# Two-block transformer-like kernel on one core: output projection and second up chunk of the second block by seven half-size products, with an up chunk's weight sums placed between the projection's additions

## The reference, cut to what matters

```python
def _layer(x, positions, g_mix, w_in, b_forget, w_branch, w_out, g_mlp, w_up, w_down):
    h = _rmsnorm(x, g_mix)
    proj = h @ w_in
    ...
    gates = jax.nn.sigmoid(gl.reshape(b, s, N_BRANCH, D_MODEL))
    y = (gates[:, :, 0, :] * (br_a @ w_branch[0])
         + gates[:, :, 1, :] * (br_b @ w_branch[1])
         + gates[:, :, 2, :] * (br_c @ w_branch[2]))
    x = x + y @ w_out                                  # 1024 x 1024: the output projection

    h2 = _rmsnorm(x, g_mlp)
    x = x + jnp.square(jax.nn.relu(h2 @ w_up)) @ w_down   # 1024 x 4096 and 4096 x 1024
    return x
```

## Time and profile before

| | us |
|---|---|
| median of 3 runs | 1498.56 (1496.29 to 1503.31) |
| the profiled execution | 1495.67, of which its span is 1493.9 |
| PE busy in the span | 1431.2 (96%) |
| DVE, ACT, POOL busy | 823.0, 328.2, 279.7 |
| mean granted TensorE clock | 0.985 of full speed |
| layer 1's branches, output projection and first two up chunks | 723.57 to 822.02 |
| the same of layer 2 | 1214.31 to 1312.77 |

### The profile page before, as it was taken

The page is one execution under the profiler, slowest core; times in us unless marked ns, Lnnn a source line. Parts: engine busy times, 40 slices in busy tenths (PEclk is TensorE's granted clock), DMA queues, the critical chain, the costliest instruction groups (busy, mean ns, idle before and its releaser), DMA issues.

```text
span 1493.9 us, 31093 instructions
## 1 busy us (share of the span) xinstructions
PE 1431.2 (96%) x13529; PEld 1279.6 (86%) x13529; DVE 823.0 (55%) x1495; ACT 328.2 (22%) x685; POOL 279.7 (19%) x144
## 2 busy tenths in 40 slices
PE   5999999989989899999999999999999999999997
PEld 2777877878778799998888999999999888899986
DVE  2345355566562666767335674544776733566553
ACT  1104023434433310143200120002014430012100
POOL 3502210000000077634000000005764400000000
PEclk8899999999989999999999999999999999999999
DMA  9533012001111464333344444446443334444451
GB/s 359 191 113 113 1 32 59 2 18 44 59 60 57 110 215 167 128 124 128 132 138 144 170 170 170 170 128 207 146 168 114 114 129 154 169 165 169 157 180 50
DMA packets 107479, 191.30 MB, mean 128 GB/s; under 512 B 8744, under 2 KB 25856, under 8 KB 107216
## 3 DMA queue, kind: packets, MB, share of 16 engines
q1 hardware_dynamic: 105968, 187.39, 36.4%
q10 hardware_dynamic: 448, 0.66, 0.2%
q0 software_dynamic: 928, 1.26, 0.2%
HBM read 187.32 MB, written 1.05 MB: 126 GB/s over the span
## 4 chain that ended last, share of the span: by engine, by line
PE 90%; DMA 2%; DVE 2%; issue 2%; ACT 1%; DVEq 1%; POOLq 1%; POOL 0%; SPq 0%; ACTq 0%
PE psum L1524 17%; PE psum L1385 15%; PE psum L1360 12%; PE psum L1521 6%; PE psum L1663 5%; PE psum L920 4%; PE psum L1644 4%; PE psum L1381 3%; PE psum L1576 2%; PE psum L993 2%; PE psum L1002 2%; PE psum L1166 2%; PE psum L1226 2%; PE psum L1445 1%; DMA arena<-in_mod_w 1%
## 5 line engine op out<-in xcount | busy, mean ns | idle before, releaser
L2111 ACT ACTIVATE arena<-psum 128x256 f32<-128x256 f32 (+7 forms) x256 | 115.1, 465 | 692.0 <-PE psum L1385 109.1
L1385 PEld LDWEIGHTS psum<-arena 128*128 128x128 f32 x2240 | 254.3, 192 | 10.8 <-issue 8.0
L1385 PE MATMUL psum<-arena 128*128 128x128 f32 x2240 | 261.2, 276 | 2.3 <-DVE arena L2720 1.2
L1524 PEld LDWEIGHTS psum<-arena 128*128 128x128 f32 x2240 | 250.4, 192 | 0.1
L1524 PE MATMUL psum<-arena 128*128 128x128 f32 x2240 | 250.5, 275 | 0.0
L1360 PE MATMUL psum<-arena 128*128 128x256 f32 x896 | 195.6, 379 | 0.0
L1360 PEld LDWEIGHTS psum<-arena 128*128 128x128 f32 x896 | 169.2, 189 | 24.7 <-issue 0.3
L873 POOL TENSOR_TENSOR arena<-arena 128x1024 f32<-128x1024 f32 x12 | 28.5, 2375 | 377.8 <-DMA arena<-in_w_in 360.9
L1521 PE MATMUL psum<-arena 128*128 128x256 f32 x448 | 97.0, 379 | 0.0
L1521 PEld LDWEIGHTS psum<-arena 128*128 128x128 f32 x448 | 84.9, 190 | 11.8
L1663 PE MATMUL psum<-arena 128*128 128x256 f32 x336 | 73.5, 380 | 1.1 <-issue 1.1
(11 more groups left out here) (403 smaller groups left out, 2008.8 us busy)
## 6 DMA issues: line engine op xcount, KB each, us to landing
arena<-in_w_in SPq DMA_DIRECT2D x31, 2048.0 KB, 8.4
arena<-in_w_up SPq DMA_DIRECT2D x16, 2048.0 KB, 8.4
arena<-in_w_down SPq DMA_DIRECT2D x16, 2048.0 KB, 8.0
arena<-in_w_out SPq DMA_DIRECT2D x6, 2048.0 KB, 7.9
arena<-in_w_branch SPq DMA_DIRECT2D x6, 2048.0 KB, 7.9
arena<-in_mod_w SPq DMA_DIRECT2D x5, 2048.0 KB, 13.7
arena<-in_w_in SPq DMA_DIRECT2D x12, 512.0 KB, 4.3
arena<-in_w_in SPq DMA_DIRECT2D x3, 1024.0 KB, 7.0
```

The costliest lines, as they stand in the source:

```text
L1385: mm = pe.matmul(b[:, n * P:(n + 1) * P], left[:, k, n * P:(n + 1) * P], right[:, k, :], start=k == 0, stop=k == half - 1)
L1524: mm = pe.matmul(b[:, n * P:(n + 1) * P], left[:, k, n * P:(n + 1) * P], right[:, k, :], start=first and n == 0 and k == 0, stop=last and ...
L2111: return act.activation(dst, src, ACT.Copy, scale=scale)
```

## The change

Four things change in each of the two layers.
1. The output projection's two chunks go by halves: 2 x 7 products instead of 4 results. Their weight sums are made by POOL, behind the gates' sums (new loop in the GpSimd block), their token sums by DVE behind the last branch addition (into `tok`). PE takes the products in the order 1, 2, 6, 5, 7, 3, 4; `out0_1` waits for `br21`, `out0_2` for `br23`, product 6 for the token sums, products 6, 7 and 3 for the weight sums.
2. ACT copies each half's first product, and DVE combines the seven results into the residual.
3. The second up chunk goes by halves too (`FIRST_SEVEN = 1`), with weight sums on DVE.
4. These weight sums (`weight_sums(0)`) no longer stand behind the token sums of `ht`, but inside the second half's additions: after those for product 7, before those for products 3 and 4.

```diff
@@ constants
-FIRST_SEVEN = 2
+FIRST_SEVEN = 1
+OUT_PRODUCTS = (1, 2, 6, 5, 7, 3, 4)
@@ GpSimd, behind the loop over the gates' chunks
+                    ly.wait_filled(gp, f"o{len(PAIRS) - 1}", l)
+                    for h in range(2):
+                        n = len(FIRST) + N_IN + 3 + h
+                        gp.wait_ge(s_slot[SLOT[n]], l * SLOT_PER_LAYER[SLOT[n]] + landed(n))
...
+                        gp.tensor_tensor(s1, w21, w22, ALU.add)
+                        gp.drain()
+                        gp.tensor_tensor(s2, s1, w11, ALU.subtract)
+                        gp.drain().then_inc(sem("out_weights_summed"), 1)
+                        gp.tensor_tensor(w21, w11, w21, ALU.subtract)
+                        gp.drain().then_inc(sem("out_weights_summed"), 1)
+                        gp.tensor_tensor(s4, w12, s2, ALU.subtract)
+                        gp.drain().then_inc(sem("out_weights_summed"), 1)
@@ TensorE
                 w = use_chunk(pe, n0 + N_IN + 3 + h, l)
-                for n in range(2):
-                    tiles(f"out{2 * h + n}", w, (2 * n * P, (2 * n + 1) * P), src=yy,
-                          ready=(lambda k: ly.wait_emptied(pe, f"br2{k // 2}", l)) if h == 0 and n == 0 else None)
+                for m in OUT_PRODUCTS:
+                    b = take_bank(ly, f"out{h}_{m}", l)
+                    if h == 0 and m < 3:
+                        ly.wait_emptied(pe, f"br2{2 * m - 1}", l)
+                    if m == 6:
+                        pe.wait_ge(sem("out_tokens_summed"), l + 1)
+                    if m in (6, 7, 3):
+                        pe.wait_ge(sem("out_weights_summed"), 3 * (2 * l + h) + (6, 7, 3).index(m) + 1)
+                    product_of_halves(b, w, m, [wsum[:, h, y] for y in range(3)], x=yy, x_sums=tok).then_inc(ly.filled, 1)
@@ ScalarE
-            norm_scalar(act, ly, "ss2", "squares2", l, done, emptied, lambda k: ly.wait_emptied(act, f"out{k // 2}", l))
+            def first_out(h):
+                ly.wait_filled(act, f"out{h}_1", l)
+                if h:
+                    ly.wait_emptied(act, "out0_7", l)
+                emptied(ly, copy(u1, bank(ly, f"out{h}_1", l)[:, 0:T], 0.5))
...
+            norm_scalar(act, ly, "ss2", "squares2", l, done, emptied, residual)
@@ VectorE
-            for n in range(4):
-                ly.wait_filled(dve, f"out{n}", l)
...
-                gained(dve, gains[1], "raw2_ready", (2 * n, 2 * n + 1))
-                if n:
-                    squares_summed(dve, done, fence, "squares2", l, (n - 1,))
-            squares_summed(dve, done, fence, "squares2", l, (3,))
+                    if (b_, n) == (2, 1):
+                        dve.tensor_tensor(tok[:, 0], token_halves(yy)[1], token_halves(yy)[0], ALU.subtract)
+            y11, y12, y21, y22 = token_halves(yy)
+            dve.tensor_tensor(tok[:, 1], y22, tok[:, 0], ALU.subtract)
+            dve.tensor_tensor(tok[:, 2], y22, y12, ALU.subtract)
+            fence()
+            dve.tensor_tensor(tok[:, 3], tok[:, 1], y21, ALU.subtract)
+            done("out_tokens_summed")
...
+            for h in range(2):
...
+                ly.wait_emptied(dve, f"{g}_1", l)
+                emptied_all(half_more(x11, product(g, 2), x11), 1)
+                emptied_all(half_more(v2, product(g, 6), v1), 1)
+                fence()
+                dve.tensor_tensor(x11, x11, v1, ALU.add)
+                p5 = product(g, 5)
+                half_more(v4, p5, v2)
+                half_more(x22, p5, x22)
+                emptied_all(half_more(v3, product(g, 7), v2), 2)
+                fence()
+                dve.tensor_tensor(x12, x12, v4, ALU.add)
+                dve.tensor_tensor(x22, x22, v3, ALU.add)
+                dve.tensor_tensor(x21, x21, v3, ALU.add)
+                fence()
+                if h:
+                    weight_sums(0)
+                    squares_summed(dve, done, fence, "squares2", l, (0, 1))
+                emptied_all(half_more(x12, product(g, 3), x12), 1)
+                fence()
+                gained(dve, gains[1], "raw2_ready", (4 * h, 4 * h + 1))
+                emptied_all(half_more(x21, product(g, 4), x21, -0.5), 1)
+                fence()
+                gained(dve, gains[1], "raw2_ready", (4 * h + 2, 4 * h + 3))
+            squares_summed(dve, done, fence, "squares2", l, (2, 3))
@@ VectorE, behind the normalised tokens
             token_sums(ht, *[tok[:, n] for n in range(4)])
-            weight_sums(0)
```

More of the change, by code:

```diff
@@ L372, in plan_layer @@
             p += [(f"o{i - 1}", "A", 1)]
-    p += [(f"br{b}{n}", "D", 1) for b in range(3) for n in range(4) if b or n] + [(f"out{n}", "D", 1) for n in range(4)]
+    p += [(f"br{b}{n}", "D", 1) for b in range(3) for n in range(4) if b or n]
+    p += [(f"out{h}_{m}", "A" if m == 1 else "D", 1) for h in range(2) for m in OUT_PRODUCTS]
     p += [("ss2", "A", 1), ("up0", "D", 1), ("up1", "D", 1)]
@@ L400 @@
 CHUNK_ENDS = (["qc1", "kf", "vc"] + [f"{x}_4" for x in HEAD_PARTS] + [f"gl{n}_4" for n in range(GATES)]
-              + [f"br{b}3" for b in range(3)] + ["out1", "out3"] + [f"up{2 * n + 1}" if n < FIRST_SEVEN else f"up{n}_4" for n in range(8)]
+              + [f"br{b}3" for b in range(3)] + ["out0_4", "out1_4"] + [f"up{2 * n + 1}" if n < FIRST_SEVEN else f"up{n}_4" for n in range(8)]
               + [None] * 3 + ["dn0_4"] + [None] * 3 + ["dn1_4"])
@@ L1513, in seven @@
                 for m in PRODUCTS:
+                    if i == 0 and m == 1:
+                        pe.wait_ge(sem("h2_ready"), l * KT + half)
                     if m == 6:
+                        if i == 0:
+                            pe.wait_ge(sem("token_sums"), 5 * l + 1)
                         pe.wait_ge(sem("weight_sums"), SEVENS * l + i + 1)
@@ L2899, in layer_vector, with weight_sums @@
             v1, v2, v3, v4 = [two_tiles(v) for v in (u1, u2, u3, u4)]
+            def weight_sums(i):
+                n = len(FIRST) + N_IN + 5 + FIRST_SEVEN + i
+                dve.wait_ge(s_slot[SLOT[n]], l * SLOT_PER_LAYER[SLOT[n]] + landed(n))
+                if SEVENS * l + i >= 2:
+                    dve.wait_ge(sem("sums_read"), SEVENS * l + i - 1)
+                s1, s2, s4 = [wsum[:, i % 2, x] for x in range(3)]
+                w11, w21, w12, w22 = quarters(ring[:, SLOT[n]])
+                dve.tensor_tensor(s1, w21, w22, ALU.add)
+                fence()
+                dve.tensor_tensor(s2, s1, w11, ALU.subtract)
+                dve.tensor_tensor(w21, w11, w21, ALU.subtract)
+                fence()
+                dve.tensor_tensor(s4, w12, s2, ALU.subtract)
+                done("weight_sums")
@@ new lines, in half_more @@
+            def half_more(dst, p, x, sign=0.5):
+                return dve.scalar_tensor_tensor(dst, p, sign, x, ALU.mult, ALU.add)
+            for h in range(2):
+                x11, x12 = [xr[:, 4 * h:4 * h + 2, r] for r in (slice(0, P), slice(P, T))]
+                x21, x22 = [xr[:, 4 * h + 2:4 * h + 4, r] for r in (slice(0, P), slice(P, T))]
+                g = f"out{h}"
+                ly.wait_emptied(dve, f"{g}_1", l)
[16 more added lines that the diff above has]
+                emptied_all(half_more(x12, product(g, 3), x12), 1)
+                fence()
+                gained(dve, gains[1], "raw2_ready", (4 * h, 4 * h + 1))
+                emptied_all(half_more(x21, product(g, 4), x21, -0.5), 1)
+                fence()
+                gained(dve, gains[1], "raw2_ready", (4 * h + 2, 4 * h + 3))
@@ L2976, in hidden_sums @@
                 token_sums(x, hid1[:, q], hid2[:, q], token_halves(x)[1], hid4[:, q])
[L2978 to L2990, removed]
-                dve.tensor_tensor(s4, w12, s2, ALU.subtract)
-                done("weight_sums")
             ly.wait_emptied(dve, "ss2", l)
```

25 lines of the change are left out of this document (11 added, 14 removed).

## The result

| | before | changed |
|---|---|---|
| median | 1497.42 us (1493.24 to 1503.31, 8 runs) | 1508.40 us (1505.56 to 1516.37, 8 runs) |
| ratio | | 1.0071, 95% interval 1.0045 to 1.0098 |
| the profiled execution | 1495.67, span 1493.9, clock 0.985 | 1516.37, span 1514.5, clock 0.979 |

The change makes the kernel slower by 0.7%, 11.0 us.

What follows compares the result with a forecast made beforehand. PE was taken to bound the kernel, busy 1431.2 of 1493.9 us. PE's work -8.1, first wait +6.4, second +6.8, clock +4.5 gave +9.6 on the median 1498.56: 1508.2 us; range 1497 to 1515.5.

Steps and rivals of the forecast that it cites:

- PE's work, -8.1: Output projection and second up chunk by halves: PE saves 4.07 us a layer, 8.1 us in both.
- First wait, 3.2 a layer: Output projection, product 6: PE waits 3.2 us a layer for token sums, as DVE's additions wait out POOL's sums.
- its list of signs: Signs in the new profile: among them, DVE's additions L2914 and L2919 to L2922 last 1 to 2.4 us, not 0.69.
- Second wait, 3.4 a layer: At ss2 (L928), PE waits 3.4 us a layer for DVE's sum of squares; bounds 2.9 to 3.8.
- What costs nothing: POOL's sums for both halves, result banks and everything behind ss2 were to add no wait.
- The cover at product 6 of the second up chunk: Behind ss2, token sums end 8.6 us after it, PE wants them 10.9 us after: 2 us cover.
- The clock, +4.5: Granted clock falls behind the new waits: four occasions of 0 to 3.0 us each, 1.5 counted, +4.5 us.
- The sum: Whole kernel: -8.1 +6.4 +6.8 = +5.1 us, with the clock +9.6, set on median 1498.56: 1508.2 us.
- -0.7 to +5: Rival: POOL's sums miss the token sums, first wait 0.3 instead of 3.2; 1498 to 1503 us; chance 0.12.
- -1.7 without the clock: Rival: the ss2 wait does not come, the first does; -1.7 us, 1497; chance 0.05.
- -7.5: Rival: neither wait comes, gain of the seven products kept; -7.5 us, 1491, faster; chance 0.08.
- both waits with the clock at full speed: Rival: both waits come, the clock stays; +5.1 us, 1503.7; chance 0.22.

Runs made afterwards that it cites:

- the run with the projection alone: Kernel before with only the output projection by halves, POOL's second group of sums behind the token sums: 1491.01 us, ratio 0.9967.
- The runs with one part alone: Kernel before with only the output projection by halves (1491.01 us, 0.9967), or only the second up chunk, weight sums behind the last sum of squares (1495.81 us, 0.9986).
- POOL out of the way: Changed kernel, POOL's second group of sums held until the output projection's token sums are done: 1496.12 us, ratio 0.9996; repeated 1500.04 us, 1.0022.
- The squares in time: Changed kernel with the second up chunk's weight sums moved behind the last sum of squares: 1495.55 us, ratio 0.9997.
- Both together: Changed kernel, POOL's second sums behind the token sums and up chunk's weight sums behind the last sum of squares: 1489.13 us, ratio 0.9942; repeated 1491.42 us, 0.9968.
- the run with the weight sums in their old place: Changed kernel with POOL's second sums held back and the up chunk's weight sums behind the token sums of h2: 1503.95 us, ratio 1.0042.

## Why the prediction was right

1508.2 us was predicted and 1508.4 measured, slower by 0.7%. By its own steps:

- *PE's work, -8.1.* Right in kind, 0.8 too large. The two chunks of the projection cost 25.45 us, not 25.01, so that its share is 2.3 us a layer (38.33 of the 66.06 in the earlier trace rows are the branches' 176 records, by the chain of the run with the projection alone), and the up chunk's 1.35 (188.95 before, 187.60 after, both with all chunks by halves that follow): -7.3 in both layers. The runs with one part alone gave -4.2, with 0.47 us of wait in it, and -2.4: -7.0 without that wait.
- *First wait, 3.2 a layer.* 3.3 and 2.9 measured, for the cause given. Set on the same start of the branches, POOL's last sum ended at 770.9, within the 770.2 to 771.4 worked out, and product 6 started at 773.3, within 772.2 to 773.4. The steps of the prediction lengthen only the first sum behind the last branch addition, its list of signs all three; the second and third took 0.68 and 0.69, so the steps were right and the list was not.
- *Second wait, 3.4 a layer.* 3.50 and 3.56 measured; the four additions are its cause, as the run without them there shows. DVE's order was as worked out: weight sums 801.53 to 806.50, squares done at 811.82, `ss2` at 811.99.
- *What costs nothing.* Held: no wait for banks, for the second half's weight sums, or behind `ss2`. The cover at product 6 of the second up chunk was called 2 us; with the weight sums put there, their 5.1 us overran it by 2.9.
- *The clock, +4.5.* Mis-sized, 6.8 in the profiled layers and 6.6 in the mean over all executions (26.8 less 20.2). It fell on three of four occasions and not on one and a half, at 1.7 or 3.4 us each and not 3.0.
- *The sum.* -7.3 + 6.25 + 7.06 + 6.8 = +12.8 for the profiled layers, which measured +12.7; predicted +9.6. The medians differ by 11.0 in the first comparison and by 16.7 in the second (6 runs of the changed kernel). So the two waits and their causes were foreseen, but that 1508.2 lies so close to 1508.4 is luck. Two terms were off the same way, by 0.8 and 2.3; the base 1498.56, a median of 3 runs, lay 1.1 above the median of 8, which hid as much; and the runs of a median scatter by more.
- *Rivals.* The runs made three of the four come true; both waits with the clock at full speed were seen in none of the changed kernel's two profiles. POOL out of the way gave +5.1 in the layers and no change or +0.2% in the time, against -0.7 to +5. The squares in time gave +1.6 in the layers and no change, against -1.7 without the clock. Both together gave 7.5 and 5.0 us less than the kernel before, against -7.5.

## What to carry to other kernels

When PE's work is cut by half a per cent, the sums that replace it must go where their engine really idles: DVE idled 2.75 us ahead of the reciprocal in the run with the weight sums in their old place, and in the second half it had no idle time between the additions of products 7, 3 and 4. A helper engine that reads SBUF costs nothing only while the other engine's additions of two SBUF operands are not urgent, so order the helper behind the urgent ones rather than start it as early as its data allow. And when you add a wait of PE, allow for the clock behind it: here 13.3 us of waits brought 6.8 us of clock in both profiles of the changed kernel. It is an average and no fixed price, as the last section shows.

## What the hardware showed that I had not expected

- Each fall of the granted clock in the changed part cost 1.7 or 3.4 us, and the same wait of 3.5 us cost the one or the other: held-back POOL lost 3.4 in layer 1 and 1.7 in layer 2 in one execution, and 1.7 and 3.4 in the next. Behind the token sums it fell in layer 1, after waits of 1.21 to 1.36 and 2.09, and not in layer 2, after 1.21 and 1.73 or 1.74, in all four profiles that have these waits. In code that is the same in all kernels, such waits can cost nothing. The wait of 3.48 us before 501.59 of the earlier trace rows, from which the prediction took its 3.0 us, stands in all fourteen profiles: it cost 3.2 to 3.4 us in twelve of them, 1.7 in one and nothing in one, the first with POOL held back.
- Unchanged code makes most of the scatter between executions (1489.6 to 1506.1 for the kernel before). The layer 1 piece measured here began anywhere between 717.66 and 737.22 us, in fourteen profiles and with no order by kernel. One of the places is in the first block. DVE and POOL there, before:

```profile
148.05 0.69 DVE L2449 TENSOR_TENSOR arena<-arena 128x512 f32<-128x512 f32 x1
148.66 0.69 DVE L2451 TENSOR_TENSOR arena<-arena 128x512 f32<-128x512 f32 x1
149.43 2.67 DVE L2453 SCALAR_TENSOR_TENSOR arena<-arena 128x512 f32<-128x512 f32 x1
```

```profile
148.78 2.77 POOL L842 TENSOR_TENSOR arena<-arena 128x1024 f32<-128x1024 f32 x1 [12.28 <-DMA arena<-in_w_in]
```

and after:

```profile
148.12 2.64 DVE L2485 TENSOR_TENSOR arena<-arena 128x512 f32<-128x512 f32 x1
150.68 2.83 DVE L2487 TENSOR_TENSOR arena<-arena 128x512 f32<-128x512 f32 x1
153.60 2.66 DVE L2489 SCALAR_TENSOR_TENSOR arena<-arena 128x512 f32<-128x512 f32 x1
```

```profile
147.60 2.61 POOL L844 TENSOR_TENSOR arena<-arena 128x1024 f32<-128x1024 f32 x1 [11.04 <-DMA arena<-in_w_in]
```

The same three instructions, once one of them slow and once all three. In all fourteen profiles the first slow one is the first that DVE starts after POOL has started its own first sum, even where only 0.01 to 0.04 us lie between the two starts. POOL starts when a transfer of weights has landed, and this differs against DVE's work from one execution to the next, of one and the same kernel too. With all three slow (seven profiles) PE waits 3.3 to 3.6 us, with two slow (one) 1.94, with one slow (six) not at all. The clock behind these waits is again not certain: it cost 3.4 us in two of the seven, the changed kernel's profile among them, and nothing in the other five. In the first profile of the changed kernel PE comes out of the wait with the granted clock at 0.50:

```profile
157.12 3.36 PE L1687 MATMUL psum<-arena 128*128 128x256 f32 x7 [3.48 <-DVE arena L2327]
```

```profile
156.00:158.00 2.00, 0.88 (x2) 0.79 (x3) 1.70 (x4) 0.00 (x0) 2.00 (x1) 0.50 0.00 0
```

and in its second at 1.00:

```profile
153.73 6.54 PE L1687 MATMUL psum<-arena 128*128 128x256 f32 x29 [3.32 <-DVE arena L2327]
```

```profile
154.00:156.00 2.00, 2.00 (x11) 1.74 (x11) 1.82 (x4) 0.00 (x0) 1.08 (x1) 1.00 0.00 0
```

What decides whether the clock falls behind a wait of this length, the runs do not show.
